# Padding the rows of the tiles that TensorE streams, in a two-block float32 kernel

## The reference

```
# first block, two layers
x = x + mixers(rmsnorm(x)) @ w_out                     # SSD, short convolution, sparse attention
u = rmsnorm(x) @ w_up;  g, v = causal_conv3(u)         # 2 x 2,752 features
x = x + (silu(g) * v) @ w_down

# second block, two layers, with a second stream of 256 context tokens xc
x  = x  + 0.5 * m[2] * swiglu(norm(x)  * (1 + m[1]) + m[0], w_in, w_out)     # half a feed-forward
xc = xc + 0.5 * ...                                                           # the same weights
x, xc = attention over both streams (latent attention, then window attention)
x  = x  + 0.5 * m[8] * swiglu(...)                                            # the other half
```

## Time and profile before

| | |
|---|---|
| median of 3 runs | 2365.93 us (2365.44 to 2366.08) |
| span of the profiled execution | 2362.4 us |
| TensorE busy | 2277.7 us, 96% |
| VectorE busy | 1698.7 us, 72% |
| ScalarE busy | 949.3 us, 40% |
| DMA queue of SyncE | 43.0% of 16 engines' span |
| mean granted TensorE clock | 0.996 |

### The profile page before, as it was taken

One profiled execution on the slowest core, in us unless ns is written; L12 is line 12 of the kernel. 1 busy time (PEld: TensorE's weight loads), 2 busy tenths in 40 slices (PEclk: granted clock), 3 DMA queues, 4 the chain that ended last, 5 costly groups with the idle time before them and its releaser, 6 DMA issues.

```text
span 2362.4 us, 35452 instructions
## 1 busy us (share of the span) xinstructions
PE 2277.7 (96%) x14536; PEld 2023.4 (86%) x14536; DVE 1698.7 (72%) x2765; ACT 949.3 (40%) x1403; POOL 114.1 (5%) x77
## 2 busy tenths in 40 slices
PE   6999998899999999999989999999999999999998
PEld 6789998799998888888768888888888888879997
DVE  6779977889989858845344884784895673696764
ACT  4766635756552222235543221212322222475342
POOL 0010010010010000010001000001000001001001
PEclk9999999999999999999999999999999999999999
DMA  6435475345455545532111454454354453313443
GB/s 253 159 128 184 154 249 198 126 179 189 163 184 181 189 156 179 186 122 81 50 72 36 161 190 140 160 185 137 123 201 158 141 175 103 130 50 126 179 155 113
DMA packets 66514, 356.91 MB, mean 151 GB/s; under 512 B 7088, under 2 KB 10160, under 8 KB 42032
## 3 DMA queue, kind: packets, MB, share of 16 engines
q1 hardware_dynamic: 66352, 354.65, 43.0%
HBM read 353.57 MB, written 1.05 MB: 150 GB/s over the span
## 4 chain that ended last, share of the span: by engine, by line
PE 84%; DVE 10%; ACT 4%; issue 1%; DMA 0%; SPq 0%; DVEq 0%; ACTq 0%
PE bank L468 84%; DVE sb_w_lo L1902 3%; ACT sb_w_hi L1239 2%; DVE sb_swS L2743 1%; DVE sb_products L1913 1%; DVE sb_swP L2757 0%; DVE sb_latP L2648 0%; DMA sb_raw<-w_l_in 0%; ACT sb_latP L1239 0%; ACT sb_nP L1239 0%; DVE sb_normed L2007 0%; DVE sb_h_lo L1984 0%; ACT sb_mid L1239 0%; DVE sb_rstd L1961 0%; ACT sb_latPT L1239 0%
## 5 line engine op out<-in xcount | busy, mean ns | idle before, releaser
L1902 DVE TENSOR_TENSOR sb_w_lo<-sb_raw,sb_w_hi 128x2048 fp32r<-128x2048 f32 (+3 forms) x289 | 586.9, 2031 | 154.8 <-ACT sb_w_hi L1239 151.8
L1239 ACT ACTIVATE sb_w_hi<-sb_raw 128x2048 fp32r<-128x2048 f32 (+3 forms) x289 | 492.5, 1704 | 391.8 <-PE bank L468 387.8
L468 PE MATMUL bank<-sb_h_hi,sb_w_hi 128*128 128x512 f32 (+1 forms) x1400 | 511.5, 365 | 8.1 <-DVE sb_w_lo L1902 7.0
L468 PE MATMUL bank<-sb_h_lo,sb_w_hi 128*128 128x512 f32 (+1 forms) x1400 | 507.3, 362 | 0.0
L468 PE MATMUL bank<-sb_h_hi,sb_w_lo 128*128 128x512 f32 (+1 forms) x1400 | 507.2, 362 | 0.0
L1913 DVE CUSTOM_DVE_ANT_0 sb_products<-sb_raw,sb_cond,sb_params 128x1024 f32<-128x1024 f32 x284 | 365.2, 1286 | 33.1 <-DVEq L1915 16.5
L468 PE MATMUL bank<-sb_f_hi,sb_w_hi 128*128 128x256 f32 (+1 forms) x1122 | 368.2, 328 | 4.3 <-DVE sb_w_lo L1902 3.9
L468 PE MATMUL bank<-sb_f_lo,sb_w_hi 128*128 128x256 f32 (+1 forms) x1122 | 366.4, 327 | 0.0
L468 PE MATMUL bank<-sb_f_hi,sb_w_lo 128*128 128x256 f32 (+1 forms) x1122 | 366.4, 327 | 0.0
L468 PEld LDWEIGHTS bank<-sb_h_hi,sb_w_hi 128*128 128x128 f32 x1400 | 264.0, 189 | 53.1 <-DVE sb_w_lo L1902 9.0
L468 PEld LDWEIGHTS bank<-sb_h_lo,sb_w_hi 128*128 128x128 f32 x1400 | 264.1, 189 | 41.2 <-issue 0.5
(11 more groups left out here) (304 smaller groups left out, 3246.0 us busy)
## 6 DMA issues: line engine op xcount, KB each, us to landing
sb_raw<-w_mod SPq DMA_DIRECT2D x144, 512.0 KB, 3.2
sb_raw<-w_l_up SPq DMA_DIRECT2D x44, 1024.0 KB, 4.8
sb_raw<-w_l_in SPq DMA_DIRECT2D x26, 1024.0 KB, 5.2
sb_raw<-w_l_down SPq DMA_DIRECT2D x32, 704.0 KB, 4.1
sb_raw<-w_m0a_up SPq DMA_DIRECT2D x22, 1024.0 KB, 4.8
sb_raw<-w_m0b_up SPq DMA_DIRECT2D x22, 1024.0 KB, 4.8
sb_raw<-w_m1a_up SPq DMA_DIRECT2D x22, 1024.0 KB, 4.8
sb_raw<-w_m1b_up SPq DMA_DIRECT2D x22, 1024.0 KB, 4.8
```

Source lines behind the costliest of these rows:

```text
L468: return nc.tensor.matmul(out, lhsT, rhs, start=start, stop=stop, skip_group_check=True)
L1239: return nc.scalar.activation(out, in_, func, **kw)
L1902: V.tensor_tensor(split_part(name, n, w_lo[s]), landed_part(name, n, raw[raw_slot(name, n)]), split_part(name, n, w_hi[s]).bitcast(F32), A ...
```

## The change

Rows get unread elements behind them: 2 in h_wide (514), 2 in h_thin (258), 4 in f with 512 columns (516), 2 in f with 256 (258). In h and in the thin f, row k starts 8k bytes further from a multiple of 1,024 bytes than row 0 does; in the wide f, 16k. The low half starts 64 bytes off the high one in h, and 192 bytes in f. What is streamed stays 256 or 512 elements of each row. `normed` takes the pitch of the wide f too. The tiles that share H and M are moved along with it: `raw_in` stands 128 bytes further than before, M too, and everything behind M 512 bytes (`raw_end` among it). `raw_last`, in the first part of H, stays, and so do H and the weight buffers.

```diff
+ROW_H, ROW_HX = 2 * T + 2, T + 2
+ROW_F, ROW_FX = 2 * T + 4, T + 2
+H_PART, HX_PART, F_PART = (4 * n + 31 & ~31 for n in (KD * ROW_H, KD * ROW_HX, HALF_FF * ROW_F))
...
-        bytes_at[0] += 32768
-        h_wide = [sb(f"h_{n}", [P, KD, 2 * T], F32R, at=H + 16384 * i) for i, n in enumerate(("hi", "lo"))]
-        h_thin = [sb(f"hx_{n}", [P, KD, T], F32R, at=H + 8192 * i) for i, n in enumerate(("hi", "lo"))]
-        raw_in = [sb(f"raw_{n}", [P, KD - 1, RAW_W], F32R, at=H + 16384 + 7232 * i) for i, n in enumerate(("hi", "lo"))]
...
+        bytes_at[0] += 2 * H_PART
+        h_wide = [sb(f"h_{n}", [P, KD, ROW_H], F32R, at=H + H_PART * i)[:, :, 0:2 * T] for i, n in enumerate(("hi", "lo"))]
+        h_thin = [sb(f"hx_{n}", [P, KD, ROW_HX], F32R, at=H + HX_PART * i)[:, :, 0:T] for i, n in enumerate(("hi", "lo"))]
+        H2 = H + 2 * HX_PART
+        raw_in = [sb(f"raw_{n}", [P, KD - 1, RAW_W], F32R, at=H2 + 7232 * i) for i, n in enumerate(("hi", "lo"))]
...
         M = bytes_at[0]
-        bytes_at[0] += 4 * 22 * 512
-        f_hi = sb("f_hi", [P, HALF_FF * 512], F32R, at=M)
-        f_lo = sb("f_lo", [P, HALF_FF * 512], F32R, at=M + 4 * HALF_FF * 512)
-        mid = sb("mid", [P, 22 * 512], at=M)
-        normed_f = sb("normed", [P, KD, 2 * T], at=M)
+        bytes_at[0] += 2 * F_PART
+        f_wide = [sb(f"f_{n}", [P, HALF_FF, ROW_F], F32R, at=M + F_PART * i)[:, :, 0:2 * T] for i, n in enumerate(("hi", "lo"))]
+        f_thin = [sb(f"fx_{n}", [P, 2 * HALF_FF, ROW_FX], F32R, at=M + F_PART * i)[:, :, 0:T]
+                  for i, n in enumerate(("hi", "lo"))]
+        mid = sb("mid", [P, F_PART // 2], at=M)
+        normed_f = sb("normed", [P, KD, ROW_F], at=M)[:, :, 0:2 * T]
...
-        def hidden(half, N):
-
-            return half[:, :].rearrange("p (n t) -> p n t", t=N)
+        def hidden(N):
+
+            return f_wide if N > T else f_thin
```

More of the change, by code:

```diff
@@ L240, in two_blocks @@
         H = bytes_at[0]
-        bytes_at[0] += 32768
-        h_wide = [sb(f"h_{n}", [P, KD, 2 * T], F32R, at=H + 16384 * i) for i, n in enumerate(("hi", "lo"))]
-        h_thin = [sb(f"hx_{n}", [P, KD, T], F32R, at=H + 8192 * i) for i, n in enumerate(("hi", "lo"))]
-        raw_in = [sb(f"raw_{n}", [P, KD - 1, RAW_W], F32R, at=H + 16384 + 7232 * i) for i, n in enumerate(("hi", "lo"))]
-        ropet = sb("ropet", [P, 2, 2 * T], at=H + 16384)
-        cbT = sb("cbT", [P, GROUPS, 384], at=H + 20480)
-        tpos = sb("tpos", [P, CMP_BLOCK * N_CMP + 20], at=H + 23552)
+        bytes_at[0] += 2 * H_PART
[3 more added lines that the diff above has]
+        raw_in = [sb(f"raw_{n}", [P, KD - 1, RAW_W], F32R, at=H2 + 7232 * i) for i, n in enumerate(("hi", "lo"))]
+        ropet = sb("ropet", [P, 2, 2 * T], at=H2)
+        cbT = sb("cbT", [P, GROUPS, 384], at=H2 + 4096)
+        tpos = sb("tpos", [P, CMP_BLOCK * N_CMP + 20], at=H2 + 7168)
         tpos_of = tpos[:, 0:CMP_BLOCK * N_CMP].rearrange("p (c i n) -> p c i n", c=2, i=CMP_BLOCK // 2)
-        kvr = sb("kvr", [P, T], at=H + 25600)
-        kvv = sb("kvv", [P, T], at=H + 28672)
-        sct = sb("sct", [P, 2, T], at=H + 26624)
+        kvr = sb("kvr", [P, T], at=H2 + 9216)
+        kvv = sb("kvv", [P, T], at=H2 + 12288)
+        sct = sb("sct", [P, 2, T], at=H2 + 10240)
         M = bytes_at[0]
-        bytes_at[0] += 4 * 22 * 512
-        f_hi = sb("f_hi", [P, HALF_FF * 512], F32R, at=M)
-        f_lo = sb("f_lo", [P, HALF_FF * 512], F32R, at=M + 4 * HALF_FF * 512)
-        mid = sb("mid", [P, 22 * 512], at=M)
-        normed_f = sb("normed", [P, KD, 2 * T], at=M)
+        bytes_at[0] += 2 * F_PART
[4 more added lines that the diff above has]
+        normed_f = sb("normed", [P, KD, ROW_F], at=M)[:, :, 0:2 * T]
         first_squares = sb("first_squares", [P, KD, T], at=M + 16384)
@@ L281, in two_blocks @@
         nPT = sb("nPT", [P, 2, 512], at=A + 8192)
-        decays = [sb(f"decays{i}", [P, 2, 384], at=H + at) for i, at in enumerate((16384, 29696))]
+        decays = [sb(f"decays{i}", [P, 2, 384], at=H2 + at) for i, at in enumerate((0, 13312))]
         latP = sb("latP", [P, 2, 2, 512], at=A)
@@ L334, in two_blocks @@
         lat_hi = sb("lat_hi", [P, 6, 512], F32R, at=M)
-        lat_lo = [sb(f"lat_lo{i}", [P, 3, 512], F32R, at=H + 16384 * i + 10240) for i in range(2)]
+        lat_lo = [sb(f"lat_lo{i}", [P, 3, 512], F32R, at=H + H_PART * (i + 1) - 3 * 4 * 512) for i in range(2)]
         key_rope, at = region(6 * 512, 512)
@@ L348, in two_blocks @@
         swPT = sb("swPT", [P, 2, 2, 512], at=M + 8192)
-        sq_q, at = region(KD * 2 * T, 8, T)
+        sq_q, at = region(KD * ROW_F, 8, T)
         sq_qrot, at = region(at, 8, T)
@@ L607, in down_by_stream @@
                 sums = norm_by_stream()
-                f = [hidden(x, 2 * T) for x in (f_hi, f_lo)]
+                f = hidden(2 * T)
                 def tile(m, w, k, at, s=0):
@@ L653, in down @@
                 b = take("res_done", KD)
-                f = [hidden(x, N) for x in (f_hi, f_lo)]
+                f = hidden(N)
                 per = 2 * T // N
@@ L1425, in ffn1 @@
                 g = take("gate_ready", FF1_TILES)
-                fh = hidden(f_hi, T)
+                fh = hidden(T)[0]
                 w0 = PARAMS[f"ffn_conv{l}"][0]
@@ L2107, in ffn1 @@
                 w0 = PARAMS[f"ffn_conv{l}"][0]
-                fh, fl = hidden(f_hi, T), hidden(f_lo, T)
+                fh, fl = hidden(T)
                 def product(n):
@@ L2206, in up2 @@
                 mb = take("ff_mid", count)
-                fh, fl = hidden(f_hi, N), hidden(f_lo, N)
+                fh, fl = hidden(N)
                 def tile(n, ahead):
```

## The result

The change makes the kernel slower: 2389.59 us (median, 2386.36 to 2390.07) against 2366.01 us, a ratio of 1.0103 [1.0091, 1.0115]. The profiled execution took 2390.07 us with a span of 2388.3 us, 25.9 us above the one before. In every run that has both, the time is 1.8 us above its span, as here; the 3.5 us named ahead of the prediction are that and 1.7 us by which the execution profiled before was faster than its median. So the spans differ by 25.9 us, and the medians only by 23.6.

A forecast was written before the change was run, and what follows sets the result against it. TensorE's start-to-start distance was taken to bound the kernel; -5 us thin, +20.8 us wide and 0 for moved tiles gave +15.8 us, rounded to +14: 2380 us, 0.6% slower. Range 2352 to 2392 us, the forecast's own 2371 to 2392.

The forecast's parts named there:

- The bound: Whole kernel: TensorE's distance from one matmul's start to the next sets the time; TensorE busy 2277.7 us, 96%.
- Term 2: 512-column matmuls on changed tiles: padding keeps them out of step, 4,530 x 4.6 ns = +20.8 us.
- The reading behind it: Dense streams: rows at one offset modulo 1,024 bytes settle into step, 13.3 ns beside their columns; padding keeps them out.
- Term 1: 256-column matmuls on changed tiles: 4,668 x -1.2 ns = -5.6 us, taken as -5 us after VectorE's cover and waits.
- Term 3: Tiles moved along, such as raw_in by 128 bytes: 2,772 padded matmuls, -3 to +3 us, taken as 0.
- The rounding: The sum of +15.8 us cut to +14, since each stage's first three matmuls and offset-0 rows may fall in step.
- Padding helps everywhere: Rival, all padded matmuls: moving offsets thin out meeting reads at any width, 9,198 x -1.2 ns = -11 us, 2355 us; chance 0.27.
- Wide stays in step: Rival: 512-column streams fall back into step within three matmuls, only the thin gain is left, 2361 us; chance 0.08.
- The change does nothing: Rival: raw_in's effect comes from its 64 bytes between halves or its place, not the pitch; 2366 us; chance 0.08.
- The excess goes away: Rival: all 13.3 ns vanish from 9,198 matmuls, 122 us less, but VectorE stops it at some 2265 us; chance 0.04.
- out of step and worse: Rival: upper bound of the wide cost plus the dearer thin price, +41 + 2 us, 2409 us; chance 0.05.
- The signs to look for: Changed profile: wide 230 to 233 ns, thin 118 to 119, 429 pieces falling to about 420, more VectorE idle before `sb_w_lo`.

The follow-up runs named there:

- Experiment 2: The change with only its 512-column rows padded, 256-column rows at their old pitch, raw_in back in place, M still 128 bytes further: 2385.22 us, ratio 1.0090.
- experiment 1: Separate kernel, TensorE streams alone, 46 layouts varying row pitch, low half's place and common shift; 512 columns: 226.7 ns at pitch 2,048, 233.0 at 2,056.
- experiment 5: Streams alone again, unpadded rows moved as a whole by 0 to 496 bytes: 226.7 to 236.7 ns with 512 columns, 113.3 to 121.7 with 256.
- experiment 6: The kernel before, unpadded, with H, M and everything behind them moved 64 bytes further: 2364.6 us, ratio 1.0000.
- experiment 3: The change with only h padded (8 bytes a row) and f unpadded, though M still stood 128 bytes further: 2389.85 us, ratio 1.0106.
- experiment 7: The change with only its 256-column rows padded, wide rows unpadded, raw_in and M still 128 bytes further: 2376.11 us, ratio 1.0048.
- experiment 8: Streams alone, weight blocks also moved, plus plain float32; 512 columns: weights moved 64 bytes 233.1 ns, both moved 226.8, plain float32 429.2 a pass.
- experiment 10: The kernel before, unpadded, with the 256-column tiles moved 192 bytes and wide tiles kept at place 0 modulo 256: 2343.43 us, ratio 0.9922.

## Why the prediction was right, and where not

- **The bound** stood. The loss is TensorE's distance from start to start; the other engines' busy times are the same, and DMA stays at 0% of the chain.
- **Term 2, the wide matmuls,** decided, with the sign forecast. Forecast +4.6 ns, measured 231.95 over all starts against 226.7: 5.25 x 4,530 = +23.8 us in place of +20.8. Experiment 2 confirms it alone (+21.8 us for the wide rows and what they move).
- **The reading behind it was wrong in its cause.** The prediction said that unpadded rows settle into step *because they all start at one offset*, and that padding keeps them out. In experiments 1, 5 and 6 unpadded rows with one offset run at 228.9 to 236.7 ns and stay there, if that offset is another one than the weights'. In the kernel before they stood at the one good place in 256 bytes. Padding by 8 or 16 bytes a row leads the stream through many places, nearly all of them dearer. That the price of a start after a pause (231.3) was so near 231.95 is not explained by this, and no run tested that transient; as far as the runs show, the good number was luck, since the layouts of experiments 1 and 5 could as well have cost 228.9 or 236.7.
- **Term 1, the thin matmuls,** had the sign right and most of the size: -0.9 ns a matmul in place of -1.2 where both traces are dense and at full clock, and -4.7 us in place of -5.6 with the waits (-2.8 as the two traces stand, since 1.9 us on hx are the lower clock). The weak step is the one that took the raw rows' 118.8 ns as the price of their *layout*. It was the price of their layout at their place: the same rows, moved by 128 bytes, cost 120.0.
- **Term 3, what is moved along,** was put at 0 with bounds of 3 us. The raw rows cost +2.8 us and the latent tiles, which it did not name, +0.8 us, together a little over the bound. This was the term to look at harder, since experiments 3 and 7 show what a move of 128 bytes alone can do: 7.9 and 9.2 us on the wide f. In the change itself f is padded too and pays that price only once.
- **The rounding** from 15.8 down to 14 had no ground: the first matmuls of a stage are not cheaper (at pitch 2,056 experiment 1 has 233.0 ns over all 144 starts and over the last 48). With all three terms at their measured size the sum is -4.7 + 23.8 + 3.6 = +22.7 us, beside 23.6 between the medians. 2380 was 9.6 us too low; the measured 2389.59 lies inside the forecast's own range of 2371 to 2392, near its upper end. Two slips changed nothing: the rows of the changed tiles are the first, second, third, fifth and sixth of the earlier trace rows and not the first five, and its counts use these; and only 1.8 of the 3.5 us between span and median are start and end of the launch.
- **The rivals.** "Padding helps everywhere" was to decide below 227.8 ns, and the wide average is 231.95. "Wide stays in step" falls by the same number. "The change does nothing" named the right cause, the place and not the pitch, and drew the wrong time from it, since padding changes the place. "The excess goes away" and "out of step and worse" fall by the wide average too, which is neither 213 nor 235.7. The Trainium skill (SBUF — State Buffer, Who interferes with whom) has TensorE read through two independent ports without ever waiting; the 226.7, 233.1 and 226.8 ns of experiment 8, with rows and weights moved apart and together, speak against it for the split form: by two independent ports, moving the weights alone would have changed nothing.
- **The signs to look for.** Wide 230 to 233 on average: yes, in distances of 227 to 236 ns that repeat every 24 matmuls. Thin 118 to 119: 119.6 for f, a little above. A fall from 429 to 420 pieces in 716 to 813: 425 there, because the wide stage now begins at 717.36 and thin pieces fill the first 1.36 us; in the purely wide 93 us it is 412 to 402. VectorE's idle time before `w_lo` grew, from 154.8 to 157.6 us.

## What to carry to other kernels

If TensorE's chain is dense and of the split float32 form, read the distance from start to start for each width and each tile, and treat the address of a streamed row, less that of the weight block, modulo 256 bytes, as a parameter of its own: here it was worth 1% either way, with the best value another one for 512 columns (0) than for 256 (192). A change of one tile's pitch or size moves everything behind it, so an experiment on one tile must hold the others' places, or it measures two things. Price a layout only by a row of the same layout at the same place, and even that left 0.9 ns open here (232.4 and 233.3). Before a span is compared with a span, read the granted clock over the whole of both: here 5.1 of 25.9 us fell where one of the two, or both, were at the lower level.

## What the runs showed of the hardware

- Back-to-back matmuls of the split form at 512 columns take 226.7 ns at best and up to 237.9 (rows moved by 4 bytes), at 256 columns 113.3 to 122.2, and the value hangs on the streamed row's place less the weights', modulo 256 bytes. TensorE was alone in these runs, so it isn't contention with another engine.
- 113.3 is exactly half of 226.7, and 226.7 is 13.3 above 512 columns at 0.417 ns each (213.3), the step between the two widths at place 0.
- Plain float32 takes 429.2 and 215.8 ns a pass for 512 and 256 columns in all five layouts tried. The Trainium skill (TensorE: Matmul & The Clock Gate, Back-to-back issue gap) gives N/2.4 + 2.5 ns for an isolated matmul. An estimate from it with two clocks a column is 429.2 and 215.8 ns, as measured; at one clock a column it is 215.8 and 109.2, which no layout of the split form reached. For a dense stream of weight loads and matmuls the same section gives about 131 ns at 512 columns, and no run here comes near that.
- Some places have two steady paces for 256 columns, 113.3 and 117.8 ns, and a stream keeps the one it falls into over its 144 matmuls. With the rows moved, place 64 (64 or 320 bytes) gave 113.3 twice and 117.8 six times in experiments 1, 5 and 8, place 192 (192 or 448 bytes) 113.3 six times and 117.8 once, less clear-cut for place 64 than the text before experiment 10 has it. With 512 columns, place 128 gave 232.4 and 233.3 ns in the kernel (experiments 3 and 7).
- At the lower clock level, hx matmuls started 215 ns apart (changed kernel, 471.23 to 472.09 us), against 120 ns at the upper one.

Left open: which part of the chip has the period of 256 bytes, why the price at a place is what it is, and what picks one of the two paces. The runs only show that the place of the one operand against the other's decides, in the split form.
